# A conditioning row spread by TensorE, early first products, and five weight chunks at another address, in a hybrid decoder layer on one Trainium2 core

## The reference

```
c_act = silu(c)
mod = (c_act @ w_ada + b_ada).reshape(B, 3, 3, D)
h = modulate(rms_norm(x, norm_ffn1), mod[:, 0, 0], mod[:, 0, 1])
x = x + 0.5 * mod[:, 0, 2] * swiglu(h, w_ffn1_in, w_ffn1_out)
h = modulate(rms_norm(x, norm_mix), ...)   # pooling mixer and latent attention
x = x + mod[:, 1, 2] * (merged @ w_out)
h = modulate(rms_norm(x, norm_ffn2), ...)
x = x + 0.5 * mod[:, 2, 2] * swiglu(h, w_ffn2_in, w_ffn2_out)
```

## Time and profile before

| | |
|---|---|
| median of three executions | 1067.24 us (1066.86 to 1069.26) |
| the profiled execution | 1066.83 us |
| its span, first to last instruction | 1065.0 us |
| around the span | 1.83 us |
| PE busy | 1037.0 us, 97% of the span |
| DVE busy, ACT busy | 537.1 us (50%), 374.3 us (35%) |
| DMA in the first 27 us | 352 GB/s |

### The profile page before, as it was taken

How to read it: one execution, slowest core, us unless ns; L and a number is a source line. 1 busy time by engine, 2 the same in 40 slices (tenths; PEclk the granted TensorE clock), 3 DMA queues, 4 the chain that set the end, 5 groups by cost and what they waited for, 6 DMA issues and landing times.

```text
span 1065.0 us, 12725 instructions
## 1 busy us (share of the span) xinstructions
PE 1037.0 (97%) x4990; PEld 877.5 (82%) x4990; DVE 537.1 (50%) x754; ACT 374.3 (35%) x522; POOL 62.0 (6%) x56
## 2 busy tenths in 40 slices
PE   2999999999999999999999999999999999999998
PEld 2888888888888899898888887898888888888887
DVE  5765656555664265777675555564333333232221
ACT  6633232232321234577544533333323223221211
POOL 0000000000000000820100003200000000000000
PEclk9999999999999999999999999999999999999999
DMA  9765454545564332223121122213222222223222
GB/s 352 298 237 202 177 217 163 228 160 200 205 236 150 115 113 93 82 80 114 45 79 50 70 79 88 93 59 114 84 95 102 83 114 79 94 81 103 88 91 96
DMA packets 28879, 138.64 MB, mean 130 GB/s; under 512 B 3248, under 2 KB 3504, under 8 KB 21168
## 3 DMA queue, kind: packets, MB, share of 16 engines
q1 hardware_dynamic: 28848, 138.23, 35.8%
HBM read 136.12 MB, written 2.10 MB: 130 GB/s over the span
## 4 chain that ended last, share of the span: by engine, by line
PE 93%; DVE 2%; ACT 1%; DMA 1%; issue 1%; POOL 1%; SPq 1%; DVEq 0%; ACTq 0%; POOLq 0%
PE bank L459 31%; PE bank L461 30%; PE bank L460 30%; DMA ada_first<-w_ada 1%; PE bank L840 1%; POOL h L2038 1%; ACT w_hi L929 0%; PE bank L790 0%; DVE k_lo L1777 0%; DVE tanh_mla L1845 0%; PE bank L514 0%; ACT h_hi L958 0%; DVE h_lo L1417 0%; SPq L412 0%; PE bank L479 0%
## 5 line engine op out<-in xcount | busy, mean ns | idle before, releaser
L459 PE MATMUL bank<-h_hi,w_hi 128*128 128x512 f32 (+1 forms) x976 | 373.4, 383 | 5.1 <-DVE h_lo L1537 2.8
L461 PE MATMUL bank<-h_lo,w_hi 128*128 128x512 f32 (+1 forms) x976 | 370.8, 380 | 0.0
L460 PE MATMUL bank<-h_hi,w_lo 128*128 128x512 f32 (+1 forms) x976 | 370.8, 380 | 0.0
L1342 DVE TENSOR_TENSOR w_lo<-w_raw,w_hi 128x2048 fp32r<-128x2048 f32 (+3 forms) x93 | 189.8, 2041 | 147.5 <-ACT w_hi L929 147.5
L459 PEld LDWEIGHTS bank<-h_hi,w_hi 128*128 128x128 f32 x976 | 184.4, 189 | 40.6 <-DVE h_lo L1537 3.2
L461 PEld LDWEIGHTS bank<-h_lo,w_hi 128*128 128x128 f32 x976 | 184.2, 189 | 35.1
L460 PEld LDWEIGHTS bank<-h_hi,w_lo 128*128 128x128 f32 x976 | 184.5, 189 | 33.9
L929 ACT ACTIVATE w_hi<-w_raw 128x2048 fp32r<-128x2048 f32 (+3 forms) x93 | 158.7, 1707 | 121.2 <-PE bank L461 77.8
L459 PE MATMUL bank<-act_hi,w_hi 128*128 128x512 f32 (+1 forms) x374 | 141.1, 377 | 0.0
L460 PE MATMUL bank<-act_hi,w_lo 128*128 128x512 f32 (+1 forms) x374 | 140.8, 377 | 0.0
L461 PE MATMUL bank<-act_lo,w_hi 128*128 128x512 f32 (+1 forms) x374 | 140.8, 376 | 0.0
(11 more groups left out here) (196 smaller groups left out, 887.3 us busy)
## 6 DMA issues: line engine op xcount, KB each, us to landing
w_raw<-w_ffn_in SPq DMA_DIRECT2D x41, 1024.0 KB, 4.8
ada_raw<-w_ada SPq DMA_DIRECT2D x56, 512.0 KB, 5.2
w_raw<-w_ffn_out SPq DMA_DIRECT2D x32, 704.0 KB, 4.0
w_raw<-w_mix SPq DMA_DIRECT2D x19, 1024.0 KB, 4.8
ada_first<-w_ada SPq DMA_DIRECT2D x16, 512.0 KB, 12.7
w_raw<-w_ffn_in SPq DMA_DIRECT2D x6, 512.0 KB, 12.8
x_tok<-x_rows SPq DMA_DIRECT2D x4, 512.0 KB, 7.2
x<-x_t SPq DMA_DIRECT2D x4, 512.0 KB, 5.6
```

The source lines that it names most:

```text
L459: nc.tensor.matmul(dst, a_hi, b_hi, start=start, stop=False)
L460: nc.tensor.matmul(dst, a_lo, b_hi, start=False, stop=False)
L461: return nc.tensor.matmul(dst, a_hi, b_lo, start=False, stop=stop)
L1342: nc.vector.tensor_tensor(w_lo[slot][:, 0:size], w_raw[slot][:, 0:size], w_hi[slot][:, 0:size].bitcast(F32), ALU.subtract).then_inc(lo_don ...
```

## The change

Four things are done.

1. `c` is loaded as one row (`c_row`, 4 KB, now the first DMA, ahead of `const_sb`). PE multiplies it with a row of ones (`one_row`, made by DVE's first instruction) in two float32 matmuls of 512 columns, into banks 0 and 1, and ACT's silu reads each half from there into `c_wide`. The 512 KB load is gone.
2. `part(0, 0)` becomes `part_high_first(0, 0)`: the four products that read `h_hi` wait for `h_hi` alone (`first_h`), and the two that read `h_lo` come last and wait for `h_ready`.
3. DVE makes `first_low(0)` before `scale_tile(1)`, not after it.
4. The five chunks that meet products of 256 columns are written to and read from `late_hi`, `late_lo`, `spare_w_hi` and `spare_w_lo`, which lie over the same slots 64 bytes further on. To make room, `w_lo` moves up by 128 bytes, and everything placed after it by 256.

The core of the diff:

```diff
@@ placements
+        late_hi = [place(f"late_hi{i}", [P, SLOT], F32R, at=cursor[0] + 4 * SLOT * i + 64) for i in range(2)]
         w_hi = [place(f"w_hi{i}", [P, SLOT], F32R) for i in range(2)]
+        cursor[0] += 128
+        late_lo = [place(f"late_lo{i}", [P, SLOT], F32R, at=cursor[0] + 4 * SLOT * i + 64) for i in range(2)]
         w_lo = [place(f"w_lo{i}", [P, SLOT], F32R) for i in range(2)]
+        cursor[0] += 128
...
+        c_row = place("c_row", [1, D], at=scaled_at)
+        one_row = place("one_row", [1, P], at=scaled_at + 8192)
...
+        spare_w_hi = place("spare_w_hi", [P, SLOT], F32R, at=w0_at + 4 * SLOT + 64)
+        spare_w_lo = place("spare_w_lo", [P, SLOT], F32R, at=w0_at + 8 * SLOT + 64)
@@ SyncE
+            sp.dma_start(c_row[:, :], c_rows).then_inc(c_in, 16)
             sp.dma_start(const_sb[:, :], consts).then_inc(const_in, 16)
-            sp.dma_start(c_wide[:, :], c_rows).then_inc(c_in, 16)
@@ TensorE
+                def part_high_first(c, k):
+
+                    cols = [slice((gu * KD + k) * P, (gu * KD + k + 1) * P) for gu in range(2)]
+                    pe.wait_ge(first_h, 2 * k + 1)
+                    pe.wait_ge(first_lo[c], k + 1)
+                    for gu in range(2):
+                        dst = bank[first_banks[c][gu]][:, :]
+                        nc.tensor.matmul(dst, first_w_hi[c][:, cols[gu]], h_hi[:, k, :], start=True, stop=False)
+                        nc.tensor.matmul(dst, first_w_lo[c][:, cols[gu]], h_hi[:, k, :], start=False, stop=False)
+                    pe.wait_ge(h_ready, k + 1)
+                    for gu in range(2):
+                        nc.tensor.matmul(bank[first_banks[c][gu]][:, :], first_w_hi[c][:, cols[gu]], h_lo[:, k, :],
+                                         start=False, stop=False)
...
-                    part(0, 0)
+                    part_high_first(0, 0)
...
-                    hi, lo = ((w_hi[0], w_lo[0]), (w0_hi, w0_lo))[s]
+                    hi, lo = ((late_hi[0], late_lo[0]), (spare_w_hi, spare_w_lo))[s]
...
-                                last = product(bank[5 + hf][:, cols], w_tile(half, k),
+                                last = product(bank[5 + hf][:, cols], late_tile(half, k),
...
-                            last = product(bank[at][:, half_cols(hf)], w_tile(slot, g * KD + k), h_pair(k, half_cols(hf)),
+                            last = product(bank[at][:, half_cols(hf)], late_tile(slot, g * KD + k), h_pair(k, half_cols(hf)),
...
+            pe.wait_ge(c_in, 16)
+            pe.wait_ge(one_row_ready, 1)
+            for half in range(2):
+                nc.tensor.matmul(bank[half][:, :], one_row[:, :], c_row[:, S * half:S * half + S], start=True, stop=True)\
+                    .then_inc(c_spread, 1)
@@ ScalarE
-            act.wait_ge(c_in, 16)
-            nc.scalar.activation(c_wide[:, :], c_wide[:, :], ACT.Silu).then_inc(c_ready, 1)
+            for half in range(2):
+                act.wait_ge(c_spread, half + 1)
+                nc.scalar.activation(c_wide[:, S * half:S * half + S], bank[half][:, :], ACT.Silu).then_inc(c_ready, 1)
@@ VectorE
                 low_part(1, 0)
+                first_low(0)
                 scale_tile(1)
-                first_low(0)
                 shift_tile(1)
```

More of the change, by code:

```diff
@@ L465, in w_tile, with late_tile @@
                 return w_hi[slot][:, cols], w_lo[slot][:, cols]
+            def late_tile(slot, t):
+                cols = slice(t * P, (t + 1) * P)
+                return late_hi[slot][:, cols], late_lo[slot][:, cols]
             def half_cols(hf):
@@ L923, in _, with split @@
         def _(act):
-            def split(pair, slot, size, used=None, spared=0):
+            def split(pair, slot, size, used=None, spared=0, hi=w_hi):
                 act.wait_ge(raw_in[slot], 16 * (pair + 1 - RAW_LATER[slot] - slot * spared))
@@ L928, in split @@
                     act.wait_ge(*used)
-                nc.scalar.activation(w_hi[slot][:, 0:size], w_raw[slot][:, 0:size], ACT.Copy).then_inc(hi_done, 1)
+                nc.scalar.activation(hi[slot][:, 0:size], w_raw[slot][:, 0:size], ACT.Copy).then_inc(hi_done, 1)
             def load_table(n, func):
@@ L1002, in mix_split @@
                 used = chunk_used[k - 2] if k >= 2 else (pe_used, FFN_CHUNKS - 1 + k)
-                split((MIX_CHUNK + k) // 2, k % 2, MIX_SIZES[k], used)
+                split((MIX_CHUNK + k) // 2, k % 2, MIX_SIZES[k], used, 0, late_hi if k == WOUT_AT + 3 else w_hi)
             def mixer():
@@ L1170, in next_high @@
                     for part in range(2):
-                        nc.scalar.activation(w_hi[0][:, n * part:n * part + n], w_raw[0][:, n * part:n * part + n], ACT.Copy)\
+                        nc.scalar.activation(late_hi[0][:, n * part:n * part + n], w_raw[0][:, n * part:n * part + n], ACT.Copy)\
                             .then_inc(hi_done if part else half_hi_done, 1)
@@ L1177, in mixer @@
                         act.wait_ge(spare_in, 16)
-                        nc.scalar.activation(w0_hi[:, 0:IN_ELEMS], w0_raw[:, 0:IN_ELEMS], ACT.Copy).then_inc(spare_hi, 1)
+                        nc.scalar.activation(spare_w_hi[:, 0:IN_ELEMS], w0_raw[:, 0:IN_ELEMS], ACT.Copy).then_inc(spare_hi, 1)
                     for g in range(2):
@@ L1266, in down @@
                         if not (last and s == 3):
-                            split((n0 + NF + s + 1) // 2 + 2 * i, (s + 1) % 2, OUT_ELEMS, (pe_used, u0 + q), f)
+                            split((n0 + NF + s + 1) // 2 + 2 * i, (s + 1) % 2, OUT_ELEMS, (pe_used, u0 + q), f,
+                                  late_hi if f == 0 and last and s else w_hi)
                         elif after:
@@ L1338, in link, with split @@
                 dve.wait_ge(small, links[0])
-            def split(n, slot, size):
+            def split(n, slot, size, hi=w_hi, lo=w_lo):
                 dve.wait_ge(hi_done, n + 1)
-                nc.vector.tensor_tensor(w_lo[slot][:, 0:size], w_raw[slot][:, 0:size],
-                                        w_hi[slot][:, 0:size].bitcast(F32), ALU.subtract).then_inc(lo_done, 1)
+                nc.vector.tensor_tensor(lo[slot][:, 0:size], w_raw[slot][:, 0:size],
+                                        hi[slot][:, 0:size].bitcast(F32), ALU.subtract).then_inc(lo_done, 1)
             def mod_tile(dst, raw, col, done):
@@ L1479, in norm_ffn2 @@
                     cols = slice(n * part, n * part + n)
-                    last = nc.vector.tensor_tensor(w_lo[0][:, cols], w_raw[0][:, cols], w_hi[0][:, cols].bitcast(F32),
-                                                   ALU.subtract)
+                    last = nc.vector.tensor_tensor(late_lo[0][:, cols], w_raw[0][:, cols],
+                                                   late_hi[0][:, cols].bitcast(F32), ALU.subtract)
                 last.then_inc(lo_done, 1)
@@ L1585, in mix_split @@
             def mix_split(k):
-                split(MIX_CHUNK + k, k % 2, MIX_SIZES[k])
+                if k == WOUT_AT + 3:
+                    split(MIX_CHUNK + k, k % 2, MIX_SIZES[k], late_hi, late_lo)
+                else:
+                    split(MIX_CHUNK + k, k % 2, MIX_SIZES[k])
             def mixer():
@@ L1929, in down @@
                         if not (last and s == 3):
-                            split(n0 + q + 1, (s + 1) % 2, OUT_ELEMS)
+                            late = f == 0 and last and s
+                            split(n0 + q + 1, (s + 1) % 2, OUT_ELEMS, late_hi if late else w_hi, late_lo if late else w_lo)
                         elif after:
@@ L1953, in ffn @@
                 down(3, True)
+            nc.vector.memset(one_row[:, :], 1.0).then_inc(one_row_ready, 1)
             nc.vector.memset(rstd[:, :], 0.0).then_inc(gu_evac, 2)
```

10 lines of the change are left out of this document (6 added, 4 removed).

## The result

The changed kernel takes 1078.21 us as the median of 5 runs (1077.74 to 1079.65), the kernel before 1067.06 in the same session: ratio 1.0102, 95% interval 1.009 to 1.0115. The forecast of 1062.8 is missed by 15.4 us and the upper end of its range, 1065.7, by 12.5, on the other side of no change.

A forecast was written before the change was run, and what follows sets the result against it. PE was taken as the bound, busy 1037.0 of 1065.0 us. 1066.83 minus 2.0 (start) minus 2.4 (halves) gave 1062.4, named as a median of 1062.8 us, range 1060.9 to 1065.7.

The forecast's parts named there:

- 390 for 512 columns everywhere: Expected profile after the change: all groups of 512-column products still record 390 ns.
- no row shows an effect of 128: Argument against a cost from moving `w_lo` by 128 bytes: the profile of the kernel before showed no such effect.
- `w_lo` at another address: Rival: `w_lo` moved by 128 bytes slows 1300 products by 7 ns each, 9.1 us more, 1071.5 us; 4%.
- the 336-column products: Counter-evidence: their moving operand alternates between 0 and 64, yet they average 154 ns, so a 64-byte shift does nothing visible.
- The rule weighed against the change: PE reads SBUF through two independent ports, so where weights start could not matter; halves give 0, 1064.8 instead of 1062.4.
- The halves: 256-column products with stationary tiles 64 bytes past: 276 instead of 283 ns, 7 ns on 345 products, 2.4 us gained.
- The extra of 331 ns: First of three 256-column score products records 331 ns; read as a start recorded early; if real, halves lose 3.8 us.
- The start: Head of the kernel: c row, high products first and DVE's new order save 2.0 us, with ends at 0.8 and 2.7.
- The two matmuls on `c_row`: Head, on PE: the row is there at 2.8, two float32 matmuls take 1.7 us each, done near 6.2.
- The cap by DVE's margins: Head: PE can gain at most 1.8 us on DVE, so its lead is cut to 1.8 + 0.4 = 2.2.
- the forecast wait of 0.5 to 1 us: Expected profile: PE waits 0.5 to 1 us in all for `h_lo` or `w_lo` before 53 us.
- The clock in the middle: Granted clock of 0.50 for 3.4 us behind 655.1, costing 1.4 us; may vanish or come twice, widening every case.

The follow-up runs named there:

- e5_both128: The kernel before with `w_hi` and `w_lo` both moved 128 bytes further, the distance between them kept; 1087.93 us, ratio 1.0189.
- e1_pad256: The changed kernel with both paddings at 256 bytes instead of 128; 1061.91 us, ratio 0.9962 to the kernel before.
- e12_order_only: The kernel before with only the high products first and DVE's new order, c loaded as before; 1065.1 us, ratio 0.9981.
- e8_late_lo192: The changed kernel with both paddings at 256 bytes and `late_lo` 192 instead of 64 bytes past `w_lo`; 1062.79 us, ratio 0.9962 to the kernel before.
- e2_start_only: The changed kernel's start (c row, high products first, DVE order) without any of its placement; 1064.48 us, ratio 0.9982 to the kernel before.
- e9_all128: The kernel before with every SBUF tile 128 bytes further, distances unchanged; 1066.63 us, ratio 0.9994.

## Why the prediction was wrong

**The step that failed** is "390 for 512 columns everywhere": the sum had no term for the 512-column products, since "no row shows an effect of 128". In the kernel before, the large tiles that these products read all stand at the same place modulo 256, so their rows couldn't show one. The runs put a term of +16 us in its place. The shift of `w_lo` was priced in a rival, "`w_lo` at another address", at 1071.5 us and 4%. That rival is what happened: putting `w_lo` back removes 16.3 us, moving it alone adds 14.0. Two things in it were off. It named the distance between high and low parts, and `e5_both128` keeps that distance and pays all the same; what counts is the distance to the moving tile. And its size was too small because it counted only the product that reads `w_lo`, 1300 x 7 ns = 9.1 us. The price of one was right (7.2 ns), but the product ahead pays too (5.7 ns), which makes 16.4.

The chance was wrong for a reason that could have been seen. The forecast took 7 ns for a shift of 64 bytes on trust from three score products, and used it for a gain. The same rows are evidence that addresses matter, and the change moved `w_lo` under three times as many products as the halves have. The trace of before even held a hint of the loss. The score products have a distance of 64, and those of 512 columns record up to 394 ns in place of 390; there are only six of that form by itself:

```profile
L460 PE MATMUL bank<-k_hi,q_lo 96*128 96x512 f32 x2 | 0.8, 394 | 0.0
```

Against it stood the 336-column products, and they still do. Their moving operand starts at 0, 64, 128 and 192 past a multiple of 256 in turn (alternately 0 and 64 past a multiple of 128, as said ahead, which makes all four), so they had all four distances in the kernel before, 128 among them. Their spacing there is 0.1539, 0.1538, 0.1541 and 0.1551 us, the same within 1.3 ns, and it stays so with `h`, their stationary side, moved. So an effect that two of three products of 512 columns pay with 6 to 7 ns isn't seen at 336, and a row of one shape says little about another. Why the width matters stays open.

**The rule weighed against the change** was that of the Trainium skill, "TensorE: Matmul & The Clock Gate", Part 2, "Step-by-step: what each phase is for": two independent read ports, so where weights start can't matter. The runs decide against this reading of it: the granted clock is 1.00 in the windows of 64 to 108 us above, and the same `h` products take 0.2265 to 0.2273 us or 0.2326 to 0.2329, by nothing but the distance of the two tiles. On that page's reading both kernels with moved tiles would have stayed at 1067.

**The halves** were forecast at -7 ns for each of 345 products, 2.4 us. Measured 6.0 ns in the changed kernel, 2 to 6 in the others. The extra of 331 ns in one of three score products was no start recorded early: its spacing to the next is 0.168 to 0.173 us in all eight attention heads, and the spacing ahead of it isn't shortened. In the halves it doesn't recur, so the +3.8 us that it might have cost stayed away. `e1_pad256` stands 2.6 us below the start alone in the same session, which looks like the forecast 2.4 and isn't: by its own spacings its halves give 345 x 2.1 ns = 0.7 us. The rest fits the clock. The profile of the start alone has two stretches at 0.50 in the middle, that of `e1_pad256` none, and three of the five executions of `e1_pad256` have a mean clock of 0.999 or 1.000, none of the ten of the start alone more than 0.998. So the gain of the halves is shown by spacings alone, 0.7 to 2.1 us, and not by a time.

**The start** was forecast at -2.0, measured -2.5 in the times and -2.1 to -2.6 at tile 2. Some of its parts agree by luck. The two matmuls on `c_row` end at 6.04, forecast 6.2, but they began 0.5 earlier than forecast (2.26 for 2.8) and took 3.78 us for 3.4. The cap by DVE's margins was placed rightly where it was reached: with 4 or 5 slow spacings (`e12_order_only`, `e1_pad256`, `e8_late_lo192`) PE waits 0.3 us for DVE's `w_lo` at tile 2. In the changed kernel and in `e2_start_only` ten slow spacings use up the lead ahead of it, and the forecast wait of 0.5 to 1 us doesn't appear. The 2.2 us that the order alone keeps look like 1.8 + 0.4 without the c row that the 0.4 stood for. But the order doesn't move DVE's list: counted from `var`, `h_lo` of tile 1 starts 11.53 us later in the kernel before and 11.61 with the order alone. That list stands 0.4 earlier only because `var` came 0.5 earlier, in a part of the head where the two kernels are the same. Against `e9_all128` the order alone keeps 1.7 at tile 2. The c row brings `var` forward: it starts at 11.5 to 11.7 in four of the five kernels that have it and at 12.08 in the fifth, against 12.10 to 12.71 with the old load. But nothing that it adds shows at tile 2 (29.74 in `e2_start_only`, 29.66 with the order alone) or in the times.

**The clock in the middle** behaved as forecast: it came once, twice or not at all, at places between 395 and 714 us, and is a few us of scatter over the runs of every kernel here.

**Three readings of the prediction** are off besides, and change nothing in the outcome. By its own terms (the halves at 10 ns, the clock drop gone) the lower end of the range is 1060.4, not 1060.9. As a median, like the forecast, the rival of `w_lo` would be 1071.9. And the slow stretch of the kernel before is six spacings of 0.427 us behind a first one of 0.59, which end at 24.38, not eight.

## What to carry to other kernels

When a change pads or moves an SBUF tile, write down for every matmul kind the distance between its stationary and its moving tile modulo 256, before and after, and count the products whose distance changes; here 1272 products of each of two kinds, at 6 to 7 ns, outweighed everything that the change was made for. For float32r matmuls of 512 columns keep the distance at 0, and pad by multiples of 256; other types weren't measured. That a trace shows no effect of something is evidence only if the thing varies in that trace, and for the shape that matters. And before a microsecond of a timeline is put down to an edit, look how much the same rows differ between kernels in which that part is the same.

## What the hardware showed that I had not expected

For float32r products of 512 columns at a granted clock of 1.00, the mean spacing of the `h` products of a kind is 0.2265 to 0.2273 us with the tiles a multiple of 256 bytes apart, 0.2322 to 0.235 at 128 (the one ahead of such a tile included), and 0.2332 to 0.2334 at 64. For 256 columns it is the other way round: 0.120 at 0, and 0.113 to 0.118 at 64, with about 0.119 at 128. For 336 columns it is 0.154 at 0, 64, 128 and 192. At one set of addresses the products of the spare chunk ran at 0.1133 us in one program and 0.1177 in another, so something besides the address decides there; what, stays open. The matmul ahead of a badly placed weight tile pays as well as the one on it. Why 256 bytes are the period, no run here tells.
